# Input rows loaded turned, the norm applied to the projected rows, and the next tile's projection dealt out by single matmuls over all eight pairs of heads

## What is computed

```
qa, ka, va, qb, kb, vb = project(rms_norm(hp, norm1_g[l]), w_in[l])
oa = attn_a_prompt(qa, ka, va, rel_bias[l])
ob = attn_b_prompt(qb, kb, vb, sinks[l])
hp = hp + merge_heads(oa, ob, out_norm_a_g[l], out_norm_b_g[l], w_out[l])
hp = hp + peer_ffn(rms_norm(hp, norm2_g[l]), w_query[l], sub_keys[l], expert_u[l], expert_v[l])
```

## Time and profile before

| | |
|---|---|
| median of 3 runs | 3794.66 us (3793.25 to 3795.22) |
| the profiled execution | 3796.45 us, its span 3794.6 us |
| PE, DVE busy | 2750.9 us (72%), 2313.9 us (61%) |
| ACT, POOL busy | 698.1 us (18%), 1091.4 us (29%) |
| mean granted TensorE clock | 0.783 |
| chain that ended last | PE 37%, DMA 35%, DVE 11%, of it gathers of experts 34% |
| projection matmuls L1136 | 287.6 us busy, x720 |

### The profile page before, as it was taken

One profiled execution on the slowest core, in us unless ns is written; L12 is line 12 of the kernel. 1 busy time (PEld: TensorE's weight loads), 2 busy tenths in 40 slices (PEclk: granted clock), 3 DMA queues, 4 the chain that ended last, 5 costly groups with the idle time before them and its releaser, 6 DMA issues.

```text
span 3794.6 us, 39042 instructions
## 1 busy us (share of the span) xinstructions
PE 2750.9 (72%) x13359; PEld 1028.7 (27%) x13359; DVE 2313.9 (61%) x6166; ACT 698.1 (18%) x2341; POOL 1091.4 (29%) x1179
## 2 busy tenths in 40 slices
PE   7999997767766766776667667666766766776665
PEld 4455544732212211221222122122212212221111
DVE  2333342747766775776677577667757766875544
ACT  2333332211112111111211111111111111111111
POOL 0000000023333333333333333333333333333332
PEclk9999998767867777776787788678778767776666
DMA  5000003259999999999999999999999999999998
GB/s 200 17 17 17 23 30 146 83 223 406 421 421 405 404 421 401 421 399 422 402 421 403 406 421 407 421 403 421 403 407 421 403 422 406 408 413 421 421 421 335
DMA packets 193446, 1277.37 MB, mean 337 GB/s; under 512 B 22624, under 2 KB 26336, under 8 KB 44384
## 3 DMA queue, kind: packets, MB, share of 16 engines
q0 software_dynamic: 167184, 1217.47, 78.1%
q1 hardware_dynamic: 26064, 57.42, 4.2%
HBM read 1255.40 MB, written 12.32 MB: 334 GB/s over the span
## 4 chain that ended last, share of the span: by engine, by line
PE 37%; DMA 35%; DVE 11%; issue 7%; ACT 6%; POOL 3%; SPq 1%; DVEq 0%; POOLq 0%; ACTq 0%
DMA arena<-in_experts,arena 34%; PE PS L1319 14%; PE PS L1136 7%; DVE arena L921 6%; PE PS L1346 5%; POOL arena L593 3%; ACT arena L801 3%; PE PS L1229 3%; PE PS L1305 2%; PE PS L1113 2%; PE PS L1218 1%; PE PS L1178 1%; ACT arena L795 1%; DVE arena L1000 1%; DVE arena L997 1%
## 5 line engine op out<-in xcount | busy, mean ns | idle before, releaser
L921 DVE CUSTOM_DVE_ANT_0 arena<-arena,PS 128x1024 f32<-128x1024 f32 x1152 | 1382.4, 1219 | 932.8 <-DMA arena<-in_experts,arena 486.7
L593 POOL DMA_INDIRECT arena<-in_experts,arena x1152 | 1082.8, 940 | 2031.4 <-PE PS L1319 1622.6
L1305 PE MATMUL PS<-arena 96*128 96x512 bf16 x2304 | 827.8, 460 | 825.4 <-DVE arena L921 778.5
L1319 PE MATMUL PS<-arena 128*32 128x512 f32 x4608 | 931.3, 952 | 111.2 <-ACT arena L801 60.2
L1305 PEld LDWEIGHTS PS<-arena 96*128 96x128 bf16 x2304 | 162.9, 104 | 1532.0 <-DVE arena L921 1278.9
L795 ACT ACTIVATE arena<-arena 128x4 f32<-128x4 f32 x288 | 59.2, 205 | 2047.3 <-DVE arena L921 2035.8
L1319 PEld LDWEIGHTS PS<-arena 128*32 128x32 f32 x4608 | 164.3, 150 | 683.9 <-issue 380.6
L1346 PEld LDWEIGHTS PS<-arena 128*128 128x128 f32 x2304 | 277.0, 200 | 86.4 <-issue 86.2
L1136 PE MATMUL PS<-arena 128*128 128x512 f32 (+1 forms) x720 | 287.6, 552 | 3.8 <-ACT arena L627 2.3
L1346 PE MATMUL PS<-arena 128*128 128x128 f32 x2304 | 290.0, 287 | 0.0
L801 ACT ACTIVATE arena<-arena 128x1 f32<-128x1 f32 x1152 | 244.8, 283 | 9.9 <-ACT arena L795 0.2
(11 more groups left out here) (129 smaller groups left out, 1579.3 us busy)
## 6 DMA issues: line engine op xcount, KB each, us to landing
arena<-in_experts,arena POOLq DMA_INDIRECT x1152
arena<-in_w_in SPq DMA_DIRECT2D x4, 2048.0 KB, 15.7
arena<-in_w_query POOLq DMA_DIRECT2D x8, 1024.0 KB, 16.9
arena<-arena SPq DMA_DIRECT2D x108, 64.0 KB
h_scratch<-arena SPq DMA_DIRECT2D x9, 512.0 KB, 2.6
arena<-h_scratch SPq DMA_DIRECT2D x9, 512.0 KB, 8.2
out<-arena SPq DMA_DIRECT2D x9, 512.0 KB
arena<-in_x_prompt SPq DMA_DIRECT2D x8, 512.0 KB, 3.5
```

Of the source, the lines that this page charges most:

```text
L593: pool.indirect_dma_start(out=uv[r], out_offset=None, in_=experts, in_offset=bass.IndirectOffsetOnAxis(ap=expert_T[t % 2][:, tok:tok + 1], ...
L921: dve.tensor_tensor_reduce(uv[r][:, 0:D], uv[r][:, 0:D], xb(n), 1.0, 0.0, ALU.mult, ALU.add, a_dot[(n // 4) % 2][:, n % 4:n % 4 + 1]).then ...
L1305: mm = pe.matmul(PS[:, 2 + 2 * (n % 2) + c, :], pick[0:96, j:j + 1].broadcast_to([96, P]), x3[t % 2][0:96, g, 512 * c:512 * c + 512], star ...
L1319: mm = pe.matmul(PS[32 * g:32 * g + 32, ACC + c, :], wz[n % 2][:, g, 31 - f:63 - f], uv[r][:, D + 512 * c:D + 512 * c + 512], start=(f == ...
```

## The change

The host gives a second copy of the rows, `xT`, already turned. SP loads tile t's 0.5 MB into the one buffer `xT` once `proj_psum` says that the tile before is projected, and POOL multiplies it by the gain (one TENSOR_TENSOR of 128x1024 for each tile, `gain`). The rows' root is no longer applied before the projection: ACT multiplies by `rstd` as it copies a projected block out of PSUM. PE's eight transposes, DVE's two evacuations L818 and its L813 are gone. The loads of `w_in` are halved, x of tile 0 comes behind the first block, and `load_turned(1)`, which waits for tile 0's projection, stands in SP's program ahead of all later loads. The 40 matmuls of a projection are dealt out by a table: ahead of `weigh` and behind `turn` of each pair.

```diff
-PIECES = range(7)
-PIECE_AT = {m: m for m in PIECES}
+PIECES = range(5)
+FILL = ((2, 4), (2, 4), (4, 2), (2, 4), (2, 2), (2, 2), (2, 2), (2, 2))
+FILL_SAMPLE = ((2, 6), (2, 6), (2, 6), (2, 6), (2, 6), (0, 0), (0, 0), (0, 0))
+def fill(t, m, behind):
+    counts = FILL if t + 1 < NT_PROMPT else FILL_SAMPLE
+    first = sum(sum(c) for c in counts[:m]) + (counts[m][0] if behind else 0)
+    return [(i // KD, i % KD) for i in range(first, first + counts[m][behind])]
+def ends(t, m, behind):
+    return [k for k, j in fill(t, m, behind) if j == KD - 1]
...
-                sp.dma_start(x_sb[0], x_prompt[0:P, :]).then_inc(x_in[0], 16)
+                def load_turned(t):
+                    if t:
+                        sp.wait_ge(proj_psum, 5 * t)
+                    sp.dma_start(xT.rearrange("p a b -> p (a b)"), xT_in[t * P:(t + 1) * P, :]).then_inc(xT_loaded, 16)
+
                 w_v = w_in.rearrange("(k p) n -> p k n", p=P)
                 sp.dma_start(g1_sb, g1).then_inc(g1_in, 16)
+                load_turned(0)
                 for c in BLOCKS:
                     cols = slice(512 * c, min(512 * c + 512, W_IN))
-                    sp.dma_start(w_in_sb[:, :, cols], w_v[:, :, cols]).then_inc(w_in_in[c], 16)
+                    for half in range(2):
+                        ks = slice(4 * half, 4 * half + 4)
+                        sp.dma_start(w_in_sb[:, ks, cols], w_v[:, ks, cols]).then_inc(w_in_in[c][half], 16)
+                    if c == BLOCKS[0]:
+                        sp.dma_start(x_sb[0], x_prompt[0:P, :]).then_inc(x_in[0], 16)
+                load_turned(1)
...
+                    if t + 2 < NT:
+                        load_turned(t + 2)
...
+                def gain(t):
+                    if t == 0:
+                        pool.wait_ge(g1_in, 16)
+                    pool.wait_ge(xT_loaded, 16 * (t + 1))
+                    pool.tensor_tensor(xT, xT, g1_sb.unsqueeze(2).broadcast_to([P, KD, P]), ALU.mult).then_inc(xT_ready, 1)
+                gain(0)
...
                 pool.wait_ge(masks, 4)
+                for t in range(1, NT):
+                    gain(t)
...
-                        act.copy(v_ring[t % V_RING], PS[:, UNIT, :]).then_inc(z_ready, 1)
+                        act.activation(v_ring[t % V_RING], PS[:, UNIT, :], ACT.Copy, scale=scale).then_inc(z_ready, 1)
...
+                        for k in ends(t, m, 0):
+                            piece(t + 1, k)
                         evacuate(t, m)
-                        if m in PIECE_AT:
-                            piece(t + 1, PIECE_AT[m])
+                        for k in ends(t, m, 1):
+                            piece(t + 1, k)
...
                     invert_rms(dve, ch, rstd[:, 0:1], ss[:, 0:1], newton[:, :, 0:1], D)
-                    dve.tensor_scalar(xn_flat, x_sb[t % 3], rstd[:, 0:1], None, ALU.mult).then_inc(xn_ready, 1)
+                    dve.sem_inc(rstd_ready, 1)
...
+                        for k, j in fill(t, m, 0):
+                            project(t + 1, k, j)
                         if m:
                             weigh(t, m - 1)
                         turn(t, m)
-                        if m in PIECE_AT:
-                            piece(t + 1, PIECE_AT[m])
+                        for k, j in fill(t, m, 1):
+                            project(t + 1, k, j)
```

More of the change, by code:

```diff
@@ L160, in build @@
 def build(nc, ins, outs):
-    (x_prompt, x_sample, ckT, cv, ckbT, cvb, g1, w_in, bias_a, bias_b, bias_s, sinks, sink_rows,
+    (x_prompt, x_sample, xT_in, ckT, cv, ckbT, cvb, g1, w_in, bias_a, bias_b, bias_s, sinks, sink_rows,
      g_ab, w_out, g2, w_query, subk, experts, gf) = ins
@@ L264, in build @@
         g1_in = sem("g1_in")
-        w_in_in = [sem(f"w_in_in{c}") for c in range(5)]
+        w_in_in = [[sem(f"w_in_in{c}_{half}") for half in range(2)] for c in range(5)]
         w_out_in = sem("w_out_in")
@@ L272, in build @@
         rms_ready = sem("rms_ready")
-        xn_ready = sem("xn_ready")
-        xT_psum = sem("xT_psum")
+        rstd_ready = sem("rstd_ready")
+        xT_loaded = sem("xT_loaded")
         xT_ready = sem("xT_ready")
@@ L611, in piece @@
                 def piece(t, k):
[L612 to L615, removed]
+                    c, scale = BLOCKS[k], rstd[:, 0:1]
+                    act.wait_ge(proj_psum, 5 * t + k + 1)
+                    if k == 0:
+                        act.wait_ge(rstd_ready, t + 1)
                     if c == 1 and t >= 5:
@@ L620, in piece @@
                     if c == 2:
-                        act.copy(v_ring[t % V_RING], PS[:, UNIT, :]).then_inc(z_ready, 1)
+                        act.activation(v_ring[t % V_RING], PS[:, UNIT, :], ACT.Copy, scale=scale).then_inc(z_ready, 1)
                     elif c == 4:
-                        act.copy(vb_ring[t % VB_RING], PS[:, UNIT, P:2 * P])
-                        act.copy(z[:, 3 * AW:Z_IN], PS[:, UNIT, 0:P]).then_inc(z_ready, 1)
+                        act.activation(vb_ring[t % VB_RING], PS[:, UNIT, P:2 * P], ACT.Copy, scale=scale)
+                        act.activation(z[:, 3 * AW:Z_IN], PS[:, UNIT, 0:P], ACT.Copy, scale=scale).then_inc(z_ready, 1)
                     else:
                         at = {0: 0, 1: AW, 3: 2 * AW}[c]
-                        act.copy(z[:, at:at + AW], PS[:, UNIT, :]).then_inc(z_ready, 1)
+                        act.activation(z[:, at:at + AW], PS[:, UNIT, :], ACT.Copy, scale=scale).then_inc(z_ready, 1)
                 def queries(t):
@@ L659, in output @@
                         act.wait_ge(o_psum, 8 * t + 4 + 4 * g)
-                        act.wait_ge(xT_psum, 2 * t + 4)
                     else:
@@ L1113, in tr, with project @@
                     return pe.transpose(PS[:, bank, k * P:(k + 1) * P], src, ident)
[L1115 to L1118, removed]
+                def project(t, k, j):
+                    c = BLOCKS[k]
+                    if t == 0:
+                        if j % 4 == 0:
+                            pe.wait_ge(w_in_in[c][j // 4], 16)
+                    if j == 0:
+                        if k:
+                            pe.wait_ge(z_ready, 5 * t + k)
+                        else:
+                            pe.wait_ge(xT_ready, t + 1)
                             if t >= 2:
                                 pe.wait_ge(h_ready, 4 * (t - 1))
[L1121 to L1133, removed]
+                                pe.wait_ge(z_ready, 5 * t)
                     w = min(512, W_IN - 512 * c)
[L1135 to L1138, removed]
+                    mm = pe.matmul(PS[:, UNIT, 0:w], xT[:, j, :], w_in_sb[:, j, 512 * c:512 * c + w],
+                                   start=(j == 0), stop=(j == KD - 1))
+                    if j == KD - 1:
+                        mm.then_inc(proj_psum, 1)
                 def turn_qk(t):
@@ L1365, in _ @@
                 for k in PIECES:
-                    piece(0, k)
+                    for j in range(KD):
+                        project(0, k, j)
                 turn_qk(0)
@@ L1468 @@
         "x_sample": np.asarray(x_sample).reshape(128, 1024),
+        "xT": np.concatenate([np.asarray(x_prompt).reshape(1024, 1024), np.asarray(x_sample).reshape(128, 1024)])
+              .reshape(9, 128, 8, 128).transpose(0, 3, 2, 1).reshape(9 * 128, 1024),
         "ckT": ck.reshape(1024, 1024),
```

15 lines of the change are left out of this document (2 added, 13 removed).

## The result

The changed kernel takes 3766.73 us (median of 4, 3765.93 to 3767.34) against 3794.94 us (3793.25 to 3798.31): a ratio of 0.9924 with a 95% interval of 0.9908 to 0.9940, 28.2 us or 0.74% faster. I had forecast 36.5 us and a range of 3744 to 3773. The span of the profiled execution is 3764.5 us, 30.1 less.

What follows compares the result with a forecast made beforehand. PE's own work plus some idle time was taken to bound the tiles; +6.5 (start), -31.6 (tiles 1 to 6) and -11.4 (end of tile 7) gave -36.5 us, hence 3758.2 us, range 3744 to 3773.

Steps and rivals of the forecast that it cites:

- PE bounds the tiles, and the softmax of pairs 0 and 1 is what stood uncovered: Prompt tiles: PE busy 95% of a tile; pairs 0 and 1 had no projection block; largest wait 2.83 us at pair 0.
- the slower rival: All pairs: matmuls add to the softmax loop instead of running beside it; 86 us in all, 3844 us; chance 0.06.
- The tiles' term: Tiles 1 to 6: idle time and transposes saved, less new waits; -31.6 us in sum, 6.2 of it in tile 5.
- I take 1.0 us of new waits for a tile: Inside each tile: PE waits newly for the one bank's hand-off, mainly at pairs 1 and 6; 1.0 us.
- My bound of 3: Inside each tile: upper bound of the new waits, 3 us; the lower bound was 0.
- ACT's scaled copy: Copying projected blocks out of PSUM: costs what the plain copy does, as both read 512 columns.
- The start: Through tile 0: SP's queue stands until tile 0's projection ends, so biases land late; +6.5 us, bounds +3 and +16.
- The end of tile 7: Sample stage's DMA chain starts from tile 8's last projection block, which ends earlier; -11.4 us, lower bound of gain 3.5.
- my case: End of tile 7: the whole DMA chain moves with the last block by 11.4 us; total 3758, chance 0.68.
- the rival that only PE's 3.5 us would come: End of tile 7: the DMA chain does not follow the last block; gain 3.5 us there, total 3766; chance 0.11.
- The gain on POOL: Each tile: POOL's multiplication takes 2.3 us, has 14 us of cover and costs nothing inside the tiles.
- a rival for the time: Tile ends: DVE stands still during POOL's gain, at most 2.3 us in eight tiles, 3777; more-waits rivals together 0.09.

Runs made afterwards that it cites:

- e2: Changed kernel with matmuls in five lumps of eight behind pairs 2 to 6, turned rows and tile 8's table kept: 3794.71 us, ratio 0.9995 to the kernel before.
- e8: Changed kernel with all matmuls of the prompt tiles' table behind `turn`, none ahead of `weigh`: 3762.51 us, ratio 0.9910 to the kernel before.
- e3: Changed kernel with tile 8's projection dealt out by the same table as the other tiles: 3770.74 us, ratio 0.9931 to the kernel before.
- e5: Changed kernel with `g2` loaded once the sample's keys and values are stored, ahead of the value loads: 3762.84 us, ratio 0.9911 to the kernel before.
- e6: Changed kernel with tile 1's turned rows loaded behind the biases but ahead of `w_out`: 3755.82 us, ratio 0.9890 to the kernel before.
- e1: Changed kernel with tile 1's turned rows loaded behind all constants and `w_out`: 3758.31 us, ratio 0.9901 to the kernel before.
- e4: Changed kernel with POOL's multiplication by the gain done three times for each tile: 3774.0 us, ratio 0.9940 to the kernel before.

## Why the prediction was right, and where its terms were off

**PE bounds the tiles, and the softmax of pairs 0 and 1 is what stood uncovered: right.** With only the dealing undone (e2), tiles 1 to 6 take 26.6 us more than in the changed kernel, and the wait at pair 0 is back. That scores and matmuls would add to the softmax loop (the slower rival) fell: 0.13 us of idle time in tile 5.

**The tiles' term, -31.6 us for tiles 1 to 6, was too large: 24.6 measured** (by the starts of the norm, 105.06 to 547.10 before and 113.93 to 531.32 after: 442.04 against 417.39). The step that failed is "I take 1.0 us of new waits for a tile". The hand-off of the bank costs less than I allowed for (0.2 us at pair 1, 413.68 to 414.81 for a turn of 0.93; 0.15 at pair 6), but I counted a matmul at 0.86 us wherever it stands, and a group takes about 0.1 us more behind scores and another 0.1 ahead of scores or `weigh`. Start to start the projection's groups in tile 5 take 32.7 us where I counted 31.0. With the hand-off, 0.35, that is some 2.0 us instead of 1.0. My bound of 3 held it. Over six tiles that is about 6 of the 7.0 us missed. e8 bears the count out from the other side: with no group between scores and `weigh` the projection takes 31.3 us, and the stretch 52.6, for which I had forecast 52.7.

ACT's scaled copy does not cost what the plain one did, as I had said: with the scale taken from a column of SBUF it takes 0.69 us for 512 columns of PSUM, against 0.58 to 0.59 before. That is 0.1 us in each hand-off, as between the blocks of tile 0 (PE's wait is 0.87 us instead of 0.77).

**The start: right in kind, too small in size.** I had +6.5; by the norm at the end of tile 0 (105.06 to 113.93) it is +8.9. In e3 and e5, whose start is the same program, it is +10.2 and +10.1, so this profile shows the start rather too well. The projection of tile 0 ended at 45.4 as forecast, but the biases landed at 63.0 and not at 60.7: I had taken all bytes of the queue to be theirs, while over 45.57 to 63.00 it moved 344 GB/s, 6.0 MB for the 5.1 that I counted (5.2 by the exact sizes), so part of `w_out`, issued at 49.43, must have gone ahead of the last of `bias_b`. Tile 0 itself lost 0.6 (I had 0.5). The lower clock in it I had read from the wrong row: over the first block before (14.40 to 23.00) the granted clock reads 1.00, though its first records are long. But after the 16.77 us without work PE is at 0.54 from 66.13 to 70.00, and four records take 3.73 us where eight take 3.60 to 3.70 later. e6, which moves one load, has tile 0 done at 101.01, 4.1 us earlier than the kernel before, so the place of that load caused the whole of the late start; e1 shows that the same load can come too late as well. Which of the changes at the start (halved loads, their order, no transposes) lets PE begin at 7.96 instead of 14.40, no run separates.

**The end of tile 7: right.** 11.4 forecast, with `w_query` 46 to 47 us after `scores(7,1)` (47.8 measured, from 545.83); the last 73.2 us from the norm to `w_query` (547.10 to 620.31) became 62.3 (531.32 to 593.62), 10.9, and the whole DMA chain followed. The total can't tell my case from the rival that only PE's 3.5 us would come: its 3766 is what was measured, by chance. The rival fell with the profile, where the chain moved by 10.9, and with e3, where PE was earlier and the kernel later. One thing I had not seen: pairs 5 to 7 of tile 7, left without matmuls, wait for ACT (1.14, 2.11 and 0.46 us), and then PE's records read longer until 623 at a granted clock of 0.66 (of 2.4 GHz; so partly at the lower level of 1.2), among them 13.33 us for an output projection of 10.46. That lies under DVE's wait for `g2`, of which 7.07 us are left of 21.40.

**The gain on POOL: right.** 1.90 us where I took 2.3, hidden in the tiles. The Trainium skill's figure (GPSIMD Engine Reference, Elementwise — side-by-side cycle accounting), 2.6 cycles an element, gave an estimate of 2.2; the trace has 1.90, and that counts. The Trainium skill's port rule (SBUF — State Buffer, Who interferes with whom) agrees with the trace, which shows DVE's small operations held until POOL ends (1.84 us instead of 0.16 in e6); as a rival for the time it fell in e4, since there is slack where the gain runs.

Sum by the profiles: +8.9 - 24.6 - 10.9 = -26.6, against +6.5 - 31.6 - 11.4 = -36.5. All three terms were off to the same side, by 9.9 us together; that the total missed by only 8.3, and stayed inside the 10 us of my forecast, owes something to luck, since it holds scatter as well.

## What to carry to other kernels

When an engine is the bound and still idles, look where its filler work stands and not at how much there is: the same matmuls, in two orders, made kernels 28 us apart (the changed kernel and e2). A wait put into an in-order queue is paid by everything behind it, so a load that must wait belongs behind what is free to go and is urgent, and ahead of what is large and not. Where a stage begins with transfers, the event that releases them counts, not when the engines are done.

## What the runs showed of the hardware that I had not expected

- A group of matmuls of 128 rows takes about 0.1 us more when the matmuls of 64 rows (scores) stand ahead of it, and about 0.1 more when scores or `weigh` stand behind it: in tile 5 four take 3.43 us between transposes, 3.53 with `weigh` behind, 3.63 with scores ahead and `weigh` behind; two take 1.72, 1.81 and 1.92. Why, the runs don't say.
- ACT's copy of 512 columns of PSUM takes 0.585 us plain and as long with a constant as its scale (the queries, in the kernel before), but 0.69 with a scale for each row read from SBUF.
- While POOL multiplied 128x1024 in SBUF (1.90 us), DVE's operations on one or two columns in SBUF took 1.3 to 1.9 us instead of 0.16, and ended with it; a `reduce` with one input in PSUM and one in SBUF, begun at 64.24 beside it, took its usual 0.29.
